# Ending attention 1 a quarter earlier and computing the mix's gate tiles in the last quarter of the scan

## The reference, cut to what matters

```python
m = silu(cond) @ w_mod + b_mod                      # modulation, 12 products of 512 columns in the kernel
hx = modulate(rms_norm(x, norm1_g), sh1, sc1)       # 512 tokens;  hc: the same for 256 context tokens
q, ff, fb, i, g, aq, ak, av, ga, gb = split(project([hc, hx]))
o_hg = scan_forward(q, i, ff) + scan_backward(q, i, fb)     # 4 heads of 128, gated recurrence
o_att = softmax(q_att @ k_att.T) @ v_att                    # 8 heads of 64, 768 keys
a = (rms_norm(o_hg) * silu(g)) @ w_branch_a
b = o_att @ w_branch_b
y = (sigmoid(ga) * a + sigmoid(gb) * b) @ w_out
x = x + g1 * y
```

## Time and profile before

| | us |
|---|---|
| median of 3 runs | 2039.3 |
| lowest and highest | 2039.01, 2041.51 |
| profiled execution | 2036.74 |
| its span | 2035.4 |

### The profile page before, as it was taken

One profiled execution on the slowest core, in us unless ns is written; L12 is line 12 of the kernel. 1 busy time (PEld: TensorE's weight loads), 2 busy tenths in 40 slices (PEclk: granted clock), 3 DMA queues, 4 the chain that ended last, 5 costly groups with the idle time before them and its releaser, 6 DMA issues.

```text
span 2035.4 us, 20226 instructions
## 1 busy us (share of the span) xinstructions
PE 1765.7 (87%) x8121; PEld 1140.9 (56%) x8121; DVE 836.1 (41%) x1335; ACT 538.9 (26%) x959; POOL 120.1 (6%) x123
## 2 busy tenths in 40 slices
PE   4999799967799893888888888898988899999998
PEld 1657566645677671232323333387745478888876
DVE  3064654654633426011101111346667644444443
ACT  2024553543222322000000000223254432222221
POOL 0002121211000001000000000000100101001110
PEclk9999899967899996999999999999988799999999
DMA  8031201221504321999999999633320022322201
GB/s 315 26 104 42 83 22 63 83 83 42 160 6 172 124 83 52 380 421 422 421 422 421 421 420 421 267 100 106 87 80 1 1 83 92 115 83 83 96 29 42
DMA packets 92440, 329.38 MB, mean 162 GB/s; under 512 B 7436, under 2 KB 22716, under 8 KB 67772
## 3 DMA queue, kind: packets, MB, share of 16 engines
q1 hardware_dynamic: 84464, 312.59, 39.8%
q10 hardware_dynamic: 5932, 8.16, 1.2%
q0 software_dynamic: 1952, 7.34, 1.0%
HBM read 322.82 MB, written 4.19 MB: 161 GB/s over the span
## 4 chain that ended last, share of the span: by engine, by line
PE 66%; DMA 14%; DVE 12%; issue 4%; ACT 3%; SPq 1%; ACTq 0%; DVEq 0%
PE PS L616 21%; PE PS L717 8%; PE PS L948 8%; PE PS L374 7%; DMA ring<-in_w_exp_down_dram 6%; DMA ring<-in_w_exp_gate_dram 5%; PE PS L370 3%; PE PS L488 3%; PE PS L728 2%; PE PS L572 2%; PE PS L783 2%; DVE wR L1585 1%; PE PS L472 1%; PE PS L456 1%; DMA ring<-in_w_mod_dram 1%
## 5 line engine op out<-in xcount | busy, mean ns | idle before, releaser
L616 PE MATMUL PS<-hR,wR 128*128 128x512 f32 x1200 | 298.5, 407 | 27.2 <-DVE wR L1585 13.1
L616 PEld LDWEIGHTS PS<-hR,wR 128*128 128x128 f32 x1200 | 230.6, 194 | 91.7 <-issue 27.0
L1585 DVE TENSOR_TENSOR wR<-ring,wR 128x1024 fp32r<-128x1024 f32 (+2 forms) x142 | 161.1, 1135 | 251.6 <-ACT wR L1034 251.4
L717 PE MATMUL PS<-ring,xeT 128*64 128x512 f32 x1024 | 229.7, 598 | 39.3 <-DMA ring<-in_w_exp_gate_dram 36.9
L1034 ACT CAST wR<-ring 128x1024 fp32r<-128x1024 f32 (+2 forms) x142 | 138.3, 975 | 213.9 <-PE PS L948 126.5
L948 PE MATMUL PS<-wR,hR 128*128 128x512 f32 x768 | 176.2, 390 | 8.9 <-DVE tmp L2313 6.9
L717 PEld LDWEIGHTS PS<-ring,xeT 128*64 128x64 f32 x1024 | 76.6, 137 | 191.0 <-issue 184.6
L616 PE MATMUL PS<-xR,wR 128*128 128x512 f32 x768 | 175.3, 389 | 0.0
L948 PEld LDWEIGHTS PS<-wR,hR 128*128 128x128 f32 x768 | 143.5, 188 | 41.5 <-DVE tmp L2313 9.7
L616 PEld LDWEIGHTS PS<-xR,wR 128*128 128x128 f32 x768 | 144.1, 188 | 29.9
L717 PE MATMUL PS<-ring,hidT 128*64 128x512 f32 x512 | 115.2, 596 | 26.8 <-DMA ring<-in_w_exp_down_dram 20.9
(11 more groups left out here) (393 smaller groups left out, 2177.6 us busy)
## 6 DMA issues: line engine op xcount, KB each, us to landing
ring<-in_w_exp_gate_dram SPq DMA_DIRECT2D x64, 1024.0 KB, 13.9
ring<-in_w_exp_up_dram SPq DMA_DIRECT2D x64, 1024.0 KB, 13.7
ring<-in_w_exp_down_dram SPq DMA_DIRECT2D x64, 1024.0 KB, 11.9
ring<-in_w_mod_dram SPq DMA_DIRECT2D x12, 2048.0 KB, 8.0
ring<-in_w_in_dram SPq DMA_DIRECT2D x11, 2048.0 KB, 12.9
ring<-in_w_up_dram SPq DMA_DIRECT2D x8, 2048.0 KB, 8.8
ring<-in_w_down_dram SPq DMA_DIRECT2D x8, 2048.0 KB, 7.9
ring<-in_w_in_dram SPq DMA_DIRECT2D x9, 1024.0 KB, 5.2
```

What stands on the lines that cost most here:

```text
L616: mm = T.matmul(b, o[s][:, k, :], x[t][:, k, :], start=(k == ks[0] and j == 0), stop=(k == ks[-1] and j == 2))
L717: mm = T.matmul(b[es, ns], stat[:, 2 * kq + k, es], W.view(units[e2])[:, k, ns], start=(kq + k == 0), stop=(kq == 3 and k == 1))
L1585: V.tensor_tensor(lo, W.view(unit)[:, ks, cs], hi.bitcast(F32), ALU.subtract) \
```

## The change

- `FILL` becomes 1 step a round in the first quarter and 1, 2, 1, 2, ... in the second and third. `MODS` moves modulation 7 into the second quarter, behind 12 rounds, and 10 into the third; 11 alone stays in the last. The quarters have 13, 16, 16 and 11 rounds; attention takes 13, 24 and 14 steps, and ends in the third.
- In the last quarter the filler is new: on TensorE `gate_tiles`, the four gate tiles in sixteen pieces of six matmuls, from round 3 on, two a round, into four banks of `rest`; on ScalarE and VectorE `gate_weights`, the token parts and the weight parts of the gate tiles. On ScalarE five of the token casts are in the third quarter (`tokens_ahead`).
- The mix begins with mg tiles 0 to 3 of the first branch. The products' norm matmuls come behind the first of them. The four gate tiles lie in PSUM meanwhile and are read by ScalarE and VectorE at the mix's start. Tiles up to 7 have their weight parts in a new buffer `wRg` where attention's data was. The branch gates of the first branch go to the upper half of `uT`, not to `sg`.
- The order of loads: modulation 7 stands before b1; mg(0,0) before w_branch_a, mg(0,1) before w_branch_b. So mg(1,0) has the slots of mg(0,0).

The last three pieces of this diff are of `act` (the filler, the start of the mix) and of `dve` (the start of the mix).

```diff
-FILL = (1, 1, 1, 2)
-MODS = ((5, 6), (), (7, 8), (9, 10, 11))
+FILL = ((1,), (1, 2), (1, 2))
+MODS = ((6, (5, 6)), (12, (7,)), (6, (8, 9, 10)), (0, (11,)))
+GATE_K = (0, 1, 2, 6, 7, 3, 4, 5)
 def weave(programs, filler, n):
-    left = list(programs)
+    left, counts = list(programs), itertools.cycle(n)
     while left:
         left = [g for g in left if next(g, "end") != "end"]
-        for _ in range(n):
+        for _ in range(next(counts)):
             next(filler, None)
...
-    for br, (a, wb, rows_of) in enumerate(((3328, "w_branch_a", cols), (4352, "w_branch_b", head_cols))):
-        u += [(("wb", br), *rows_of(d[wb], 0, 1024)), (("mg", br, 0), *cols(d["w_in"], a, 512)),
-              (("mg", br, 1), *cols(d["w_in"], a + 512, 512))]
+    u += [(("mg", 0, 0), *cols(d["w_in"], 3328, 512)), (("wb", 0), *cols(d["w_branch_a"], 0, 1024)),
+          (("mg", 0, 1), *cols(d["w_in"], 3840, 512)), (("wb", 1), *head_cols(d["w_branch_b"], 0, 1024)),
+          (("mg", 1, 0), *cols(d["w_in"], 4352, 512)), (("mg", 1, 1), *cols(d["w_in"], 4864, 512))]
...
+    mix_chunks += mg[0][:4]
+    for t in range(8):
+        mix_chunks += wb[0][t:t + 1] + mg[0][t + 4:t + 5]
+    for t in range(8):
+        mix_chunks += mg[1][t:t + 1] + wb[1][t:t + 1]
...
+        def gate_tiles(pool):
+            for n in range(6):
+                yield
+            for n, (key, *_) in enumerate(mix_chunks[:4]):
+                b = pool.take(T, key, dve_mix["silu", n])
+                T.wait_ge(*dve_lo[key])
+                o = parts(wRg, mix_chunks, n)
+                for i, k in enumerate(GATE_K):
+                    if n == 0:
+                        T.wait_ge(*dve_mix["hR", k])
+                    for j, (s, t) in enumerate(TERMS):
+                        mm = T.matmul(b, o[s][:, k, :], hR1(t, k), start=(i + j == 0), stop=(i == 7 and j == 2))
+                    if i == 7:
+                        mm.then_inc(pe_mm.sem, pe_mm.up((key, 0)))
+                    if i % 2:
+                        yield
...
-        for q in range(4):
-            weave([combine(levels, q)] + ([prepare(gates, q + 1)] if q < 3 else []) + [modulation(gates, MODS[q])] +
+        for q in range(3):
+            weave([combine(levels, q), prepare(gates, q + 1), modulation(gates, *MODS[q])] +
                   ([head_norms()] if q == 2 else []), both, FILL[q])
         for _ in both:
+            pass
+        ahead = gate_tiles(rest)
+        weave([combine(levels, 3), modulation(gates, *MODS[3])], ahead, (2,))
+        for _ in ahead:
             pass
...
+        def gate_weights():
+            A.wait_ge(*dve_scan["y", 2, 6])
+            tokens((5, 6, 7))
+            yield
+            A.wait_ge(*pe_att.end)
+            copy_hi(wRg, mix_chunks, 0)
+            yield
+            copy_hi(wRg, mix_chunks, 1)
...
+            copy_hi(wRg, mix_chunks, 5)
+            gate(0)
+            gate(1)
+            gated(0)
+            gate(2)
+            gated(1)
+            gate(3)
+            copy_hi(wRg, mix_chunks, 6)
+            A.wait_ge(*dve_mix["hn", 3])
+            A.activation(sq1, sq1, ACT.Sqrt).then_inc(s.sem, s.up("rn"))
+            copy_hi(wRg, mix_chunks, 7)
...
+            gate(3)
+            for h in range(2, 4):
+                V.wait_ge(*pe_mix["hn", h])
+                V.tensor_scalar(sq1[:, h - 2, :], bank(("hn", h))[:, 0:512], 1.0 / 128, EPS, ALU.mult, ALU.add) \
+                    .then_inc(s.sem, s.up(("hn", h)))
+            sub_lo(wRg, mix_chunks, 6)
+            head(2)
+            sub_lo(wRg, mix_chunks, 7)
+            gated(2)
+            head(3)
+            sub_lo(wR1, mix_chunks, 8)
+            gated(3)
```

More of the change, by code:

```diff
@@ L1 @@
+import itertools
 from contextlib import ExitStack
@@ L219, in program @@
     m4 = Area(nc, DYN + 3120, END)
-    hR1 = [m4.take(f"hR1{i}", [128, 8, 512], F32R) for i in range(2)]
+    hR1h, hR1l = m4.take("hR1h", [128, 8, 512], F32R), m4.take("hR1l", [128, 6, 512], F32R)
+    sq1 = m4.take("sq1", [128, 2, 512])
     wR1 = m4.take("wR1", [128, 2, 2, 1024], F32R)
     aR, tm = (m4.take("aR", [128, 4, 512], F32R), aRl), m4.take("tm", [128, 512])
-    sq1 = Area(nc, KEEP + 8192, HT).take("sq1", [128, 2, 512])
+    m4 = Area(nc, KEEP + 4096, HT)
+    wRg, hR1m = m4.take("wRg", [128, 2, 2, 1024], F32R), m4.take("hR1m", [128, 2, 512], F32R)
     xk = Area(nc, KEEP, KEEP + 4096).take("xk", [128, 4, 1024])
@@ L276, in program, with hR1, mix_weights @@
     bmod = colA[:, 64:112]
+    def hR1(t, k):
+        return hR1h[:, k, :] if t == 0 else hR1l[:, k, :] if k < 6 else hR1m[:, k - 6, :]
+    def mix_weights(n):
+        return wRg if n < 8 else wR1
     lb, omlb = lbt[:, 4, :], lbt[:, 5, :]
@@ L520, in prepare, with modulation @@
             yield
-        def modulation(pool, js):
-            if not js:
-                return
-            for n in range(6 if js[-1] < 9 else 0):
+        def modulation(pool, wait, js):
+            for n in range(wait):
                 yield
@@ L1135, in mod_rows, with modulation @@
             A.copy(mrow, bank(("mod", j))).then_inc(act_mod.sem, act_mod.up(("row", j)))
-        def modulation(js):
-            if not js:
-                return
-            for n in range(6 if js[-1] < 9 else 0):
+        def modulation(wait, js):
+            for n in range(wait):
                 yield
@@ L1566, in act @@
         both = attention()
-        for q in range(4):
-            weave([combine(q)] + ([prepare(q + 1)] if q < 3 else [tokens()]) + [modulation(MODS[q])] +
-                  ([head_norms()] if q == 2 else []), both, FILL[q])
+        for q in range(3):
+            weave([combine(q), prepare(q + 1), modulation(*MODS[q])] + ([head_norms(), tokens_ahead()] if q == 2 else []),
+                  both, FILL[q])
         for _ in both:
             pass
+        weave([combine(3), modulation(*MODS[3])], gate_weights(), (1,))
+        copy_hi(wRg, mix_chunks, 4)
         mix()
@@ L2350, in head_norms, with gate_weights @@
                 yield
-        def tokens():
-            for n in range(4):
-                yield
+        def gate_weights():
+            V.wait_ge(*pool_scan["x", 2, 6])
+            for k in range(3):
+                token_low(k)
+            yield
+            V.wait_ge(*pe_att.end)
+            for k in range(6, 8):
+                token_low(k)
+            yield
+            sub_lo(wRg, mix_chunks, 0)
+            yield
             V.wait_ge(*pe_scan["ke", 3, 4])
-            for k in range(6):
+            for k in range(3, 6):
                 token_low(k)
-                yield
+            yield
+            sub_lo(wRg, mix_chunks, 1)
+            yield
+            sub_lo(wRg, mix_chunks, 2)
+            yield
+            yield
+            sub_lo(wRg, mix_chunks, 3)
+            yield
         zero = prepare(0)
@@ L2372, in dve @@
         both = attention()
-        for q in range(4):
-            weave([combine(q)] + ([prepare(q + 1)] if q < 3 else [tokens()]) + [modulation(MODS[q])] +
-                  ([head_norms()] if q == 2 else []), both, FILL[q])
+        for q in range(3):
+            weave([combine(q), prepare(q + 1), modulation(*MODS[q])] + ([head_norms()] if q == 2 else []),
+                  both, FILL[q])
         for _ in both:
             pass
+        weave([combine(3), modulation(*MODS[3])], gate_weights(), (1,))
+        sub_lo(wRg, mix_chunks, 4)
         mix()
```

195 lines of the change are left out of this document (106 added, 89 removed).

## The result

| | before | after |
|---|---|---|
| median of the runs | 2039.2 us (20 runs) | 2031.4 us (20 runs) |
| ratio, with 95% interval | | 0.9963 [0.9950, 0.9977] |
| profiled execution: own time, span | 2036.7, 2035.4 | 2033.8, 2032.5 |
| start of the third, of the last quarter | 350.7, 445.6 | 395.9, 498.0 |
| end of the scan | 521.9 | 552.3 |

What follows compares the result with a forecast made beforehand. It took the attention chain over three engines to bound the kernel from 402 us on, TensorE elsewhere. +24 - 6 - 18 - 12.8 - 17.1 (branch gates done earlier) - 4.3 = -34.2 us: 2002.5 profiled, median 2005, range 1991 to 2023.

Steps and rivals of the forecast that it cites:

- The step that failed: Second quarter: 94.5 + 9.0 of added attention work + 3.0 of waits + 19.2 for four bare rounds, 125.7 us, +24.
- The lower bound of this quarter: Second quarter: six last steps at bare work, 9.0, plus 2.4 of modulation, give 116 us.
- the links of the third quarter's last chain: Third quarter's end: scan outputs, decay, exponentials, modulations 9 and 10 with product and turns, about 15.5 us where 27.4 stood.
- Third quarter: 14 attention steps instead of 13, all in the first ten rounds: 89.0 us, -6, bounds 84 and 98.
- the old 5.00: Third quarter, 402.0 to 418.2: TensorE's wait of 5.00 us for ScalarE's table changes stays, the stretch remaining 16.2 us.
- Last quarter: Loses 12 attention steps and two of three modulations, gets four gate tiles: 58 us, -18, bounds 50 and 70.
- rival (b): Last quarter: gate weights load 10 us later than counted, ScalarE stands still, quarter 68 us, total 2015; chance 0.13.
- (d): Last quarter stays at 76 us because the levels' chain, not attention, sets its pace; total 2023; chance 0.05.
- Start of the mix: To the first branch product, which waits for VectorE's low part of head 3: 28 us, -12.8, bounds 25 and 33.
- the load of mg(1,0): Between the branches: TensorE's wait for this load goes, since its ring slots are freed long before: -4.3 us.
- (a): Paired steps lose 2.5 us each everywhere; second and third quarters take 65 us more, total 2070, slower; chance 0.07.
- (c): After gaps near the ends of quarters two and three, 12 us at 1.2 GHz cost 6 each: 2017; chance 0.12.

Runs made afterwards that it cites:

- the run with the late product: Kernel after with filler cycle 2, 1 and the product with the values moved to the first step of the next head but one: 2020.1 us, 0.9908.
- the run with added matmuls: Kernel after with 44 unread matmuls of 512 columns ahead of attention steps late in the second and third quarters: 2066.2 us, 1.0126.
- the packed cycle: Kernel after, two attention steps in the second quarter's first 11 rounds, one in its last 5 and each round of the third: 2042.9 us; with turns and product later, 1999.0.
- the run with the cycle (2, 1): Kernel after with the fill of the second and third quarters turned round, 2, 1 instead of 1, 2: 2025.2 us, 0.9927.
- The deeper order alone: Kernel before, one attention step a round, turns one step later and the product in the second step of the head after the next: 2015.6 us, 0.9868.
- the change at cycle (2, 1): Kernel after with fill 2, 1, turns one step later and the product in the second step of the head after the next: 2009.1 us, 0.9862.
- Packed: Kernel after with later turns and product, two attention steps in the second quarter's first 11 rounds, one in its last 5 and each round of the third: 1999.0 us, 0.9816.
- the late product costs the kernel before: Kernel before with only the product with the values moved to the first step of the next head but one: 2043.0 us, 1.0031.

## Why the forecast was wrong

**The step that failed.** "I take 0.5 in each of six rounds, 3 us. Then four rounds hold six steps": the second quarter. It was measured as 146.6 us, 20.9 more than forecast, and the parts are these.

- Count. `prepare` has work for TensorE in eleven rounds, not twelve, and the step of round 11 already stands behind it. Before 365.3 there are 15 attention steps, behind it 9, where I had 18 and 6. The 94.5 us of the kernel before held ten steps, so five come to them and not six. At my own prices that makes 94.5 + 5 x 1.5 + 3.0 = 105.0 and 9 x 3.2 = 28.8, where I had 106.5 and 19.2: +8.1 by the count alone.
- Dense rounds, 116.0 for 105.0. Idle time is 5.8 us where I took 3.0, which is +2.8. The rest, +8.2, is work at a lower clock: 110.2 us busy, where 94.5 + 7.5 = 102.0 was priced, and 102.3 was measured for the same work in the run with the late product. I had charged the waits and put the lower clock in dense rounds at nothing. Half of this term is no fixed price of the order: the same code took 106.0 us busy in another execution, in the run with added matmuls. The wait itself I had as 0.5 us in each pair; it was 0, 0.17, 1.98, 3.67 and 0 us, and the two long ones come from the gap exponential standing behind other work on ScalarE.
- Bare rounds, 30.6 for 28.8: +1.8. The pace of the earlier trace rows was right to 0.2 us a step.

These four, 8.1 + 2.8 + 8.2 + 1.8, are the 20.9. What the runs showed in place of the step is that a pair costs what its order lets TensorE wait: with the packed cycle the dense rounds take 155.0 us in this order and 113.7 in the deeper one.

Two small sums of the prediction do not come out as written. The lower bound of this quarter, 94.5 + 9.0 + 9.0 + 2.4, is 114.9 and not 116, and the links of the third quarter's last chain add up to 14.7, not 15.5. Neither changes the reading.

**Third quarter**, 102.1 for 89.0. Up to the sixth level (464.04; 401.95 in the kernel before) 68 us passed for 57.3. Of that +10.7, the stretch from 395.9 to 463.0 has 7.0 us idle and 60.1 busy, at 0.95 and 0.79, where the kernel before had 51.3 busy and none idle; with the three steps more, 4.5 us together, taken out, 4.3 are slow clock. The wait of 7.71 us at 474.14 is the one that I kept as the old 5.00 and that grew, since the logarithm, the root and their tables, which stood ahead of a score exponential on ScalarE, now stand ahead of a gap exponential (at 471.56), and VectorE's scaling of 2.2 us has to come behind it before the turn:

```profile
470.27 1.28 ACT L1145 ACT_TABLE_LOAD   x1
471.56 0.21 ACT L1145 ACTIVATE st<-st 128x4 f32<-128x4 f32 x1
...
472.59 1.41 DVE L1829 TENSOR_SCALAR pb<-pb,st 128x384 f32<-128x384 f32 x4
```

From the sixth level to the last chain it is 16.9 us all the same, where 16.2 was forecast. The final chain was sized well: 17.1 for 15.5.

**Last quarter**, 54.3 for 58: right, and so is the reason, 50.6 us of it busy. The gate weights were not late; rival (b) falls, and (d) with it.

**Start of the mix**, 27.0 for 28, with the VectorE wait that was forecast; the gate tiles behind it and the load of mg(1,0) too: from the first branch product to the last squares row it is 177.1 us (579.25 to 756.38), where the forecast gave 199.7 - 17.1 - 4.3 = 178.3. Half the prediction, the half with nothing about attention, is right within 4 us in each term.

**The whole.** The profiled execution took 31.3 us more than the 2002.5 forecast: 20.9 + 13.1 in the two quarters, -3.7 in the last, -1.0 and -1.2 in the mix, and 3.1 behind it (1276.1 us for 1273.0), where the change touches nothing and nothing was forecast.

**Rivals.** (a) was the right mechanism: paired steps lose time to the chain. It was priced at 2.5 us a step everywhere and turned the sign from 1.7 on; by its own count the two quarters lost (146.6 + 102.1 - 115 - 70.6) / 38 = 1.7 a step, just at the threshold, so that the sign came right by little. Of that, 20.9 + 13.1 = 34 us over 38 steps, less the 8.1 of the count, is 0.7 lost for each beyond what I had counted. It had been offered as all or nothing, and a version at half its price should have been a case of its own. (c) had the clock as a cost, but in another place: I put it at the ends of the quarters, and against what was counted it cost most in the dense rounds. The Trainium skill ("TensorE: Matmul & The Clock Gate", Part 1: The HAM clock gate) has the engine fall to half rate when idle. The stretches at 0.83 and 0.89 behind the waits of 1.98 and 3.67 us agree; the three waits of 2.3 us in the run with the cycle (2, 1), at 0.99, show that not every such wait brings it.

**What the gain is against.** Third and last quarter of the kernel before were slow from the waits of the earlier trace rows. I took them for the cost of attention without projections beside it, and the change for their cure. The deeper order alone makes both quarters shorter, and the kernel by 24 us, and on top of it the change at cycle (2, 1) is worth nothing that can be told (0.9862 [0.9843, 0.9881] and 0.9868 [0.9840, 0.9897]). Packed it may be worth another 0.5%, in intervals that just touch: 0.9816 [0.9792, 0.9840]. With that order and that cycle the two quarters take 129.7 + 85.3 = 215.0 us; 125.7 + 89.0 = 214.7 were forecast. That the two agree is in part luck: the packed cycle has 27 and 12 steps in them and not the 24 and 14 of the forecast (the deeper order has one step more). With the cycle (2, 1), 24 and 15 steps, the deeper order takes 131.8 + 94.6 = 226.4, so 22 of the 34 us are gone with the order and the cycle, and 12 are left.

What stays open: how much of the third quarter's loss is clock and how much the idle time before it, since the run with added matmuls could not part them; why some waits are followed by a lower clock and others of the same length are not; and why the late product costs the kernel before some 5 us.

## What to carry to other kernels

Where steps of a pipelined loop are issued as filler, look at what lies on the waited engine between a result and its reader once two steps fall into one round: if it is one short row, the round trip over the other engines can show (2 to 5 us here, in some of the pairs), and a reader moved one step later takes most of it away. Put the reader further back before moving the work elsewhere: here that was worth 16 us with the change at the same cycle (22 with the other cycle) and 24 without it, and the change itself 8. When an idle time of a few us is charged to a dense stretch, leave room for a slower clock behind it: 5.8 us of waits came with 4 and with 8 us of slower matmuls here, and 7.4 us, in three waits of 2.3, with 1.

## What the runs showed of the hardware

- The same two waits of TensorE, 1.98 and 3.67 us (5.8 us idle in all), came with a granted clock of 0.92 and 110.2 us busy in one execution, and with 0.95 and 106.0 in another of the same code. Three waits of 2.3 us (7.4 idle) came with 0.99 and 103.0. 27.9 us idle in 155.0 came with 0.87.
- ScalarE took its queue in order here: an exponential of 0.2 us on the critical chain, whose input was ready at 293.0, started at 297.93, behind four gate activations and a table load of 1.28. For the wait of 3.67 us it stood behind a copy that waited for the projection until 324.58, and a table load again.
- A float32 matmul over 512 columns shows as two records (44 added matmuls, 88 records); a gate tile's float32r matmuls show as one each (24 records for 24). Work that is added must be counted in records of the trace.
